# Norm weights spread over the partitions by a product with a row of ones, squares of the last tiles ahead of high halves, table products between chunks

## The reference, cut to what matters

```python
def rmsnorm(x, g):
    xf = x.astype(jnp.float32)
    y = xf * lax.rsqrt(jnp.mean(xf * xf, axis=-1, keepdims=True) + EPS)
    return (y * g.astype(jnp.float32)).astype(x.dtype)

xn = rmsnorm(x, norm_mix)
proj = xn @ w_in
q, k, v, cb, cc, ch, ga, gb = jnp.split(proj, [int(i) for i in np.cumsum(SPLITS)[:-1]], axis=-1)
...
att, kv_rows = dilated_attention(q, k, v, rel_bias, kv_bufs)
...
x = x + m @ w_o
h = rmsnorm(x, norm_mlp)
x = x + jnp.square(jax.nn.relu(h @ w_ff1)) @ w_ff2
```

## Time and profile before

| what | value |
|---|---|
| time, median of three executions | 1695.65 us (1692.61 to 1696.15) |
| profiled execution: time | 1697.69 us |
| profiled execution: span | 1695.8 us |
| TensorE busy | 1650.8 us, 97% of the span |
| VectorE busy | 672.5 us, 40% |
| ScalarE busy | 472.1 us, 28% |
| GpSimd busy | 73.1 us, 4% |
| mean granted clock of TensorE | 0.992 of full speed |

### The profile page before, as it was taken

The page is one execution under the profiler, slowest core; times in us unless marked ns, Lnnn a source line. Parts: engine busy times, 40 slices in busy tenths (PEclk is TensorE's granted clock), DMA queues, the critical chain, the costliest instruction groups (busy, mean ns, idle before and its releaser), DMA issues.

```text
span 1695.8 us, 28576 instructions
## 1 busy us (share of the span) xinstructions
PE 1650.8 (97%) x10715; PEld 1602.2 (94%) x10715; DVE 672.5 (40%) x1222; ACT 472.1 (28%) x906; POOL 73.1 (4%) x86
## 2 busy tenths in 40 slices
PE   7999999999989999999999999999999999999998
PEld 7999998888978888899999999999999999999998
DVE  6112123344644444323544344333333333333454
ACT  5212123443433443111423331033101321033212
POOL 0430000000000000000122000000000000000011
PEclk9999999999999999999999999999999999999998
DMA  5524554332256765433111111111111111111112
GB/s 174 158 90 129 172 181 123 110 103 85 82 154 171 200 175 147 148 102 108 39 50 37 50 37 50 49 37 49 50 37 49 37 49 40 46 41 46 43 31 106
DMA packets 229017, 152.08 MB, mean 90 GB/s; under 512 B 23870, under 2 KB 219286, under 8 KB 228969
## 3 DMA queue, kind: packets, MB, share of 16 engines
q1 hardware_dynamic: 200412, 120.32, 24.7%
q10 hardware_dynamic: 26268, 28.31, 4.9%
q0 software_dynamic: 2288, 2.80, 0.7%
HBM read 118.32 MB, written 35.43 MB: 91 GB/s over the span
## 4 chain that ended last, share of the span: by engine, by line
PE 86%; issue 3%; DVE 3%; DMA 3%; ACT 2%; SPq 2%; ACTq 1%; DVEq 0%; POOL 0%
PE bank L626 27%; PE bank L627 27%; PE bank L628 27%; ACT wh L1042 1%; PE bank L771 1%; PE bank L740 1%; PE bank L757 1%; PE bank L693 1%; DMA wr<-in_w_conv_out_dram 1%; PE bank L950 1%; DMA xt<-in_x_prompt_dram 1%; DMA xp<-in_x_sample_dram 0%; DMA out_dram<-yt 0%; DMA wr<-in_w_in_dram 0%; SPq L510 0%
## 5 line engine op out<-in xcount | busy, mean ns | idle before, releaser
L626 PE MATMUL bank<-xhi,wh 128*128 128x352 f32 (+1 forms) x1104 | 373.2, 338 | 4.7 <-DVE sga L1811 2.6
L627 PE MATMUL bank<-xlo,wh 128*128 128x352 f32 (+1 forms) x1104 | 362.2, 328 | 0.0
L628 PE MATMUL bank<-xhi,wl 128*128 128x352 f32 (+1 forms) x1104 | 361.8, 328 | 0.0
L1449 DVE TENSOR_TENSOR wl<-wr,wh 128x1024 fp32r<-128x1024 f32 (+1 forms) x134 | 179.7, 1341 | 260.2 <-ACT wh L1042 259.4
L627 PE MATMUL bank<-flo,wh 128*128 128x368 f32 (+1 forms) x768 | 251.7, 328 | 0.0
L627 PE MATMUL bank<-hlo,wh 128*128 128x368 f32 (+1 forms) x768 | 251.4, 327 | 0.0
L626 PE MATMUL bank<-hhi,wh 128*128 128x368 f32 (+1 forms) x768 | 250.6, 326 | 0.3 <-DVE rel L1867 0.3
L626 PE MATMUL bank<-fhi,wh 128*128 128x368 f32 (+1 forms) x768 | 250.5, 326 | 0.0
L628 PE MATMUL bank<-fhi,wl 128*128 128x368 f32 (+1 forms) x768 | 250.1, 326 | 0.0
L628 PE MATMUL bank<-hhi,wl 128*128 128x368 f32 (+1 forms) x768 | 250.1, 326 | 0.0
L1042 ACT ACTIVATE wh<-wr 128x1024 fp32r<-128x1024 f32 (+1 forms) x134 | 136.1, 1015 | 364.8 <-PE bank L628 293.4
(11 more groups left out here) (218 smaller groups left out, 1734.2 us busy)
## 6 DMA issues: line engine op xcount, KB each, us to landing
wr<-in_w_ff_dram SPq DMA_DIRECT2D x64, 512.0 KB, 3.7
wr<-in_w_in_dram SPq DMA_DIRECT2D x46, 512.0 KB, 3.9
d_T<-stg ACTq DMA_DIRECT2D x18, 544.0 KB, 2.8
kvc<-in_cache_kv_g_dram SPq DMA_DIRECT2D x16, 512.0 KB, 5.3
kvc<-in_cache_kv_g_dram SPq DMA_DIRECT2D x32, 256.0 KB, 5.8
d_tm<-tm ACTq DMA_DIRECT2D x12, 512.0 KB, 3.7
d_m<-bb ACTq DMA_DIRECT2D x8, 544.0 KB, 3.0
ml<-d_m SPq DMA_DIRECT2D x8, 544.0 KB, 4.4
```

Source lines behind the costliest of these rows:

```text
L626: pe.matmul(bank[c][:, 0:n], wh[st_.p][:, k, :], a, start=(k == 0), stop=False)
L627: pe.matmul(bank[c][:, 0:n], wh[st_.p][:, k, :], b, start=False, stop=False)
L628: last = pe.matmul(bank[c][:, 0:n], wl[st_.p][:, k, :], a, start=False, stop=(k == nk - 1))
L1449: dve.tensor_tensor(wl[st_.p][:, 0:nk, :], wr[st_.p][:, 0:nk, :], f32(wh[st_.p][:, 0:nk, :]), ALU.subtract).then_inc(w_lo, 1)
```

## The change

The transfer of the norm weights brings one row to one partition. GpSimd sets a row of ones first of all. TensorE, behind its 28 warm-up products, multiplies the row of ones with the two halves of the weights' row into banks 0 and 1, so that each partition gets the row, and runs two more warm-up products. ScalarE copies the first half back over `gb` behind the root of tile 0 and ahead of the squares of the tiles 1 and 2; VectorE copies the second half ahead of the scaling of tile 0, which waits for both copies.

On ScalarE the squares of the tiles 6 and 7 move ahead of the high halves of tile 3, and the square of tile 8 directly behind these.

The table block is cut in four: the three products of the bias table each follow one chunk of step 2, and the transposes follow the first chunk of step 3. ScalarE's copies of the table and its store move behind step 2's copies, VectorE's copies of the constants behind those of step 3.

```diff
@@ the SP queue
-                sp.dma_start(gb[:], bass.AP(g_mix.tensor, 0, [[0, P], [1, D]])).then_inc(gb_in, 16)
+                sp.dma_start(gb[0:1, :], bass.AP(g_mix.tensor, 0, [[D, 1], [1, D]])).then_inc(gb_in, 16)
@@ TensorE
-        def tables():
-            pe.wait_ge(x_lo, 2 * TILES)
+        def tables(g):
             pe.wait_ge(tab_in, 16 * 6)
             pe.wait_ge(relb_one, 1)
-            for g in range(NG):
+            if g is not None:
                 pe.matmul(bank[3 + g][0:12, 0:TABLE], relb[:], onehot[:, g * TABLE:(g + 1) * TABLE],
                           start=True, stop=True).then_inc(bt_pe, 1)
+                return
...
         keep_warm(WARM[0])
+        pe.wait_ge(gb_in, 16)
+        pe.wait_ge(ones_row, 1)
+        for half in range(2):
+            pe.matmul(bank[half][:], sr[:, 0, :], gb[0:1, 512 * half:512 * half + 512], start=True, stop=True).then_inc(gb_pe, 1)
+        keep_warm(WARM[1])
...
         chunk(Step(0), KD, 2, xhi, xlo)
-        tables()
         chunk(Step(1), KD, 2, xhi, xlo)
-        for s in range(2, 6):
+        for c in range(3):
+            chunk(Step(2), KD, c, xhi, xlo)
+            tables(c)
+        chunk(Step(3), KD, 0, xhi, xlo)
+        tables(None)
+        for c in (1, 2):
+            chunk(Step(3), KD, c, xhi, xlo)
+        for s in range(4, 6):
@@ ScalarE
         square_x(0)
         root_x(0)
+        act.wait_ge(gb_pe, 2)
+        act.activation(gb[:, 0:512], bank[0][:], ACT.Copy).then_inc(gb_c, 1)
         square_x(1)
...
         split_hi(Step(1), KD)
+        square_x(6)
+        square_x(7)
         split_x_hi(3)
-        square_x(6)
+        square_x(8)
         stage_first(0, 0, 1)
         split_x_hi(4)
-        square_x(7)
-        square_x(8)
         root_x(3)
...
         split_hi(Step(2), KD)
+        stage_first(1, 2, 6)
+        qkv_step(Step(2), d_T[0], 2, None, 0)
         act.wait_ge(bt_pe, 3)
...
-        stage_first(1, 2, 6)
-        for k in range(2, 6):
+        for k in range(3, 6):
@@ VectorE
-        dve.wait_ge(gb_in, 16)
+        dve.wait_ge(gb_pe, 2)
+        dve.tensor_copy(gb[:, 512:D], bank[1][:]).then_inc(gb_c, 1)
+        dve.wait_ge(gb_c, 2)
         scale_x(0)
...
+        for k in (2, 3):
+            qkv_step(Step(k), k, None, 0)
         dve.wait_ge(bt_pe, 4)
...
-        for k in range(2, 6):
+        for k in (4, 5):
@@ GpSimd
+        pool.memset(sr[:, 0, :], 1.0).then_inc(ones_row, 1)
+        pool.wait_ge(ones_row, 1)
         pool.memset(relb[N_BUCKETS:N_BUCKETS + 1, :], 1.0).then_inc(relb_one, 1)
```

More of the change, by code:

```diff
@@ L271, in build @@
     id_in, tab_in, gb_in, x_in = sem("identity_in"), sem("tables_in"), sem("g_mix_in"), [sem(f"x_in{t}") for t in range(TILES)]
-    root_warm = sem("root_table_loaded")
+    root_warm, ones_row, gb_pe, gb_c = sem("root_table_loaded"), sem("ones_row_set"), sem("g_mix_spread"), sem("g_mix_copied")
     relb_one, ssq_one, toe_neg, sbias_neg = sem("mask_row_set"), sem("ssq_set"), sem("toeplitz_masked"), sem("sample_bias_masked")
```

## The result

| | before | after |
|---|---|---|
| median | 1695.29 us (9 runs, 1692.61 to 1697.71) | 1700.56 us (9 runs, 1698.52 to 1703.06) |
| profiled execution: time, span | 1697.69 us, 1695.8 us | 1698.52 us, 1696.4 us |
| mean granted clock | 0.992 | 0.994 |

The changed kernel takes 1.0033 times as long, interval [1.0022, 1.0043]: +5.6 us, between +3.7 and +7.3 (the medians themselves differ by 5.3). That is more than the 0.2% (3.4 us) which counts as a difference. The prediction was +3.6 us.

The account below looks back on a forecast made before the run. The prediction took TensorE to bound the kernel, with waits or low clock only in the first 57 us. It summed 5.0 - 1.1 - 0.5 + 0.2 = +3.6 us onto 1695.65, giving 1699.3, range 1696.6 to 1701.9.

Parts of the forecast that it names:

- Part 1: Start, up to the first big product: spreading the weights by products behind the warm-up delays it by 5.0 us.
- the ramp's clock: Start, tile transposes on TensorE: lying thinner, they run partly at the lower clock, +0.2 us.
- Part 2: Step 0, tile 6: earlier squares on ScalarE let its transposes start without waiting, -1.1 us.
- Part 3: Table products cut up between chunks: seams cost, the low clock behind the block is mostly saved, sum -0.5 us.
- seams: Places where table products meet chunks on TensorE: three more places at 0.18 us each, +0.5 us.
- the lower clock: 24 products behind the table block: a slow spell worth 1.6 us, two thirds of it counted as saved, -1.0 us.
- what is moved past: Queues of ScalarE, POOL and VectorE: moved copies, store and table chain are covered by idle time or late readers, no cost.
- (a): Rival at the table block: its spell saved in full, seams free, +2.3 us, 1698.0, within 0.2%; chance 0.40.
- (b): Rival in the first chunk: the lower clock stays throughout it, about +1.5 us more, 1700.8; chance 0.12.
- (c): Rival at the start: without the 512 KB transfer tiles 1 and 2 land early, -5.6 us, 1690.0; chance 0.05.

Follow-up runs that it names:

- squares moved ahead: Changed kernel with squares and root of tiles 1 and 2 ahead of the wait for the spread, on ScalarE and VectorE: 1699.28 us, 1.0032 of before.
- pieces in the gaps: Changed kernel with the table products behind the third chunks of steps 0 and 1 and step 2's first chunk: 1696.20 us, 1.0022 of before.
- split moved ahead: Changed kernel with the high half of step 2's weights ahead of ScalarE's store issue: 1699.64 us, 1.0033 of before.

## Why the prediction was right or wrong

**Direction and range** were right: slower, and 1700.56 us lies between 1696.6 and 1701.9. The forecast of 1699.3 was 1.3 us short, and its difference of +3.6 was 2.0 short of +5.6.

**Part 1** was predicted at +5.0, and the ramp's clock at +0.2 on top; the trace shows +5.22 for both. All of it lies ahead of the root step for the tiles 1 and 2, which came at 17.54 where 17.3 was predicted: the spread's products began at 12.62 instead of 12.41, and took 1.98 us where 1.9 was taken. From there on both kernels need 8.49 us, so the clock term came to nothing, although the clock did fall in the ramp (0.53, with transposes of 1.97 us; the 1.56 that the prediction took for the lower clock stand in a stretch whose mean is 0.61); that the two terms add up to the measured 5.2 is luck. The squares of the tiles 1 and 2 were the last to come, as predicted, but only by about 1 us ahead of TensorE's own order (squares moved ahead). What the sum had as fixed was the warm-up's end. It varies by 1.3 us between executions, and the spread hands that on.

**Part 2** was predicted at -1.1 and measured at -1.22 in the pair, -1.09 alone, and 1.1 where the clock was the same. The scaling of tile 6 came in time and the transposes did not wait. In the pair some 0.4 us of the difference is the first chunk's lower clock before.

**Part 3 failed.** The prediction gave -0.5, seams at +0.5 and the lower clock at -1.0. The pair shows +1.09: seams of 0.89, waits of 1.77 us that were not in the sum, and the lower clock at -1.57 (53.12 to 58.82 and 58.82 to 78.00 both at 1.00). That last term is as large as this only because the profiled execution of before had the spell; with two of five it is some -0.6 in the mean, less than the two thirds that the prediction counted. The step that failed is the paragraph on what is moved past. It looked at the queues past which instructions move and asked what covers the moved work there. It did not ask what the block itself had covered: ScalarE's copy out of bank 2 between two chunks that both use it, and the split of step 2's weights behind it. Alone, the part is worth 1.0006 [0.9996, 1.0016]; with the pieces in the gaps the waits are gone.

**The sum of the parts** is 1.0023 - 0.0010 + 0.0006 = 1.0019 alone, and 1.0033 and 1.0037 together. One joint term is shown, the wait of 0.80 us, which takes the stop that comes with the spread and the missing block at once. It is 0.0005 to 0.0006 (0.80 in the idle column, 1.06 from the split moved ahead). The other 0.001 is as large as the intervals and is left open: by the medians the parts add up to +5.4 us, against +5.3 and +6.6 together.

**The rivals.** (a) had the block's spell saved in full, and in the pair it was; but the seams and waits took more. (b) did not come: the first chunk ran at 1.00 from 26.00 on, better than before (0.61 in its first 4.4 us). The lower clock lay ahead of it instead, 0.53 in 14.60 to 21.60, behind the spread, while TensorE was mostly turning tiles, and tile 2's transposes at 22.50 took 1.09 us, the length at the full level. The rule of the Trainium skill, "TensorE: Matmul & The Clock Gate", section "Part 4: PE-mode transpose", that transposes do not count as TensorE activity in the same way, would leave it low there; as eight warm-up instructions stand between these transposes, no run here decides on it. Nor does the spread by itself bring the low clock: with half the warm-up products ahead of the same spread it read 1.00 from 11.20 to 22.70. What decides is open. (c) is out: without the transfer altogether, the first product came 0.1 us earlier, or some 1 us with a warm-up as long as before's.

## What to carry to other kernels

When a block of work is moved out of the way, ask what stood in its shadow: the copy that frees a bank between two chunks, the split of the next weights, a slow issue. The best place for small loose work is where TensorE would wait anyway. And before a transfer is replaced by a chain over several engines, look for the engine that the consumer really waits for: here tile 0 waited for TensorE's warm-up products, so that the transfer cost about 1 us at most, and the chain behind them cost 5.2.

## What the runs showed of the hardware

The four product instructions with one weight row took 1.98 us at 12.62 and 3.77 us at 4.53, as the first work of TensorE. The 36 warm-up instructions behind the latter took 0.19 us each. In the kernel before, 56 took 0.146 each: 19 in their first 3.77 us, and the other 37 in 4.40 us, 0.12 each (0.15 with the spread alone). So in this one execution 3.77 us of these products brought TensorE less far up than as much time of warm-up products did. The granted-clock column reads 1.00 in all these stretches, so the pace can be told from the durations alone; why it differs is open. Behind the products at 12.62 the clock read 0.53 for 7 us; behind the same products at 9.31, with half the warm-up products ahead, it read 1.00.

The 56 warm-up instructions of the same program part took 8.16 to 9.44 us in different profiles. The issue of one and the same store on ScalarE took 0.41 us in the six profiles without the spread and 2.0 to 2.4 in the eight with it, and a packet of instructions lies within the long ones and some 2.5 us behind the start of the short ones.
